# A hybrid decoder layer in fp32r on one core: the ConvFFN's gate and up products by one level of Strassen's scheme, the FFN in two passes through DRAM

## What is computed

```python
h = rmsnorm(x, norm_ffn_g)
gate, new_ffn = causal_dwconv(h @ w_gate, ffn_prev, conv_ffn_w, conv_ffn_b)
x = x + (jax.nn.silu(gate) * (h @ w_up)) @ w_down
```

## Time and profile before

| | us |
|---|---|
| median of 3 runs | 2509.6 (2509.47 to 2510.82) |
| span of the profiled execution | 2507.9 |
| PE busy (matmuls) | 2462.1, 98% |
| PE weight loads busy | 2452.1, 98% |
| DVE busy | 1206.8, 48% |
| ACT busy | 617.1, 25% |
| POOL busy | 160.2, 6% |
| mean granted clock of PE | 0.992 of full |
| DMA | 219.17 MB, mean 87 GB/s |

### The profile page before, as it was taken

How to read it: one execution, slowest core, us unless ns; L and a number is a source line. 1 busy time by engine, 2 the same in 40 slices (tenths; PEclk the granted TensorE clock), 3 DMA queues, 4 the chain that set the end, 5 groups by cost and what they waited for, 6 DMA issues and landing times.

```text
span 2507.9 us, 45612 instructions
## 1 busy us (share of the span) xinstructions
PE 2462.1 (98%) x18473; PEld 2452.1 (98%) x18473; DVE 1206.8 (48%) x1902; ACT 617.1 (25%) x738; POOL 160.2 (6%) x279
## 2 busy tenths in 40 slices
PE   6999999999999999999999999999999999999996
PEld 6999999999999999999999999999999999999996
DVE  6357644556224535455434444444544354454445
ACT  6224312113113322222212222122222211222224
POOL 3310000001221000000000000000000000000004
PEclk8999999999999999999999999999999999999998
DMA  5422222224222222223222222222232222222222
GB/s 153 159 84 71 69 85 85 83 85 151 83 79 73 84 80 81 84 84 92 75 84 84 84 84 81 80 80 82 78 97 78 76 84 84 84 84 84 84 85 84
DMA packets 326837, 219.17 MB, mean 87 GB/s; under 512 B 6804, under 2 KB 301839, under 8 KB 324992
## 3 DMA queue, kind: packets, MB, share of 16 engines
q1 hardware_dynamic: 324432, 203.98, 27.2%
q0 software_dynamic: 2352, 14.41, 1.6%
HBM read 208.19 MB, written 10.18 MB: 87 GB/s over the span
## 4 chain that ended last, share of the span: by engine, by line
PE 96%; ACT 1%; DVE 1%; POOL 0%; issue 0%; DMA 0%; POOLq 0%; SPq 0%; DVEq 0%; ACTq 0%
PE ps L1161 32%; PE ps L1163 31%; PE ps L1162 31%; DVE h_lo L797 0%; POOL acc L470 0%; ACT ps L540 0%; PE ps L1284 0%; ACT h_hi L512 0%; PE ps L1297 0%; DMA x_nat<-in_x_prompt_dram 0%; ACT X L520 0%; PE ps L1296 0%; ACT w_hi L491 0%; DVE rms L813 0%; PE ps L1276 0%
## 5 line engine op out<-in xcount | busy, mean ns | idle before, releaser
L1161 PE MATMUL ps<-h_hi,w_hi 128*128 128x288 f32 x4608 | 1362.2, 296 | 6.2 <-issue 4.9
L1163 PE MATMUL ps<-h_hi,w_lo 128*128 128x288 f32 x4608 | 1358.7, 295 | 0.0
L1162 PE MATMUL ps<-h_lo,w_hi 128*128 128x288 f32 x4608 | 1358.3, 295 | 0.0
L1161 PEld LDWEIGHTS ps<-h_hi,w_hi 128*128 128x128 f32 x4608 | 865.6, 188 | 8.4 <-issue 5.8
L1162 PEld LDWEIGHTS ps<-h_lo,w_hi 128*128 128x128 f32 x4608 | 865.7, 188 | 0.0
L1163 PEld LDWEIGHTS ps<-h_hi,w_lo 128*128 128x128 f32 x4608 | 865.7, 188 | 0.0
L771 DVE TENSOR_TENSOR w_lo<-raw,w_hi 128x1024 fp32r<-128x1024 f32 x376 | 460.5, 1248 | 305.7 <-ACT w_hi L491 305.6
L491 ACT ACTIVATE w_hi<-raw 128x1024 fp32r<-128x1024 f32 x376 | 384.2, 1050 | 489.9 <-PE ps L1163 474.5
L1161 PE MATMUL ps<-act_hi,w_hi 128*128 128x288 f32 x1408 | 418.4, 297 | 1.0 <-DVE scaled L781 1.0
L1163 PE MATMUL ps<-act_hi,w_lo 128*128 128x288 f32 x1408 | 415.0, 295 | 0.0
L1162 PE MATMUL ps<-act_lo,w_hi 128*128 128x288 f32 x1408 | 414.3, 294 | 0.0
(11 more groups left out here) (184 smaller groups left out, 921.6 us busy)
## 6 DMA issues: line engine op xcount, KB each, us to landing
raw<-in_w_gate_dram SPq DMA_DIRECT2D x88, 512.0 KB, 3.9
raw<-in_w_up_dram SPq DMA_DIRECT2D x88, 512.0 KB, 3.8
raw<-in_w_down_dram SPq DMA_DIRECT2D x88, 512.0 KB, 4.3
raw<-in_w_in_dram SPq DMA_DIRECT2D x80, 512.0 KB, 4.3
raw<-in_w_out_dram SPq DMA_DIRECT2D x32, 512.0 KB, 4.0
xT_scratch<-X POOLq DMA_DIRECT2D x1, 4608.0 KB, 18.5
X<-xT_scratch POOLq DMA_DIRECT2D x4, 1152.0 KB, 5.6
x_nat<-in_x_prompt_dram SPq DMA_DIRECT2D x4, 1024.0 KB, 8.6
```

Source lines behind the costliest of these rows:

```text
L1161: te.matmul(out, whi, xhi, start=start, stop=False)
L1162: te.matmul(out, whi, xlo, start=False, stop=False)
L1163: return te.matmul(out, wlo, xhi, start=False, stop=stop)
```

## The change

The FFN falls into two passes. Pass 1 computes gate and up of all 44 tiles and stores silu(gate)·up, split into hi and lo, in DRAM (`act_scratch`). Pass 2 reads that back in four chunks of 8, 12, 12 and 12 tiles and does the whole down projection: 24 groups of two output tiles, each over one chunk, and a last round over the fourth chunk that is interleaved with the final norm.

- **Tiles 0 to 3 of pass 1** are computed as before (`first_quad`, `std_quad`). h is now normalised fully before it is split: the sum of squares, the root, a reciprocal per half of the rows, then x·g·rb in place, the copy to hi and the subtraction. While these tiles run, DVE and ACT make the differences of row halves and contraction halves that the scheme needs, hi and lo, in `hq`, `tq` and in the place of X. X itself goes to DRAM first (`x2_scratch`, one DMA of POOL for each of its 16 rows) and comes back for the down projection.
- **Tiles 4 to 43** take one level of the Strassen-Winograd scheme over (gate, up) x (even, odd contraction tiles) x (row halves): 7 products of 8 steps and 3 matmuls, 168 matmuls of 128x288 for a gate and up tile, where it was 192 (`quad`, `product`). DVE adds four sums of weight pieces of 128x1024 (`sum1` to `sum4`), so that a tile has 7 pieces to split and 4 sums, from 4 loaded pieces. Intermediate sums of the outputs go through `snap` and `up_sum`.
- **The loads of a tile** are four of 512 KB: gate even and odd into `raw`, up even and odd into `raw_c` and `raw_d`. The two gate loads of the next tile wait until product 4 of this one has been split (both its buffers are in use up to there), the third until product 5, the fourth until product 6. In memory a piece now takes every second contraction tile (`wpart`), again in segments of 512 bytes.
- **POOL** stores each tile's activations (576 KB) with a DMA, in the same queue as its copies of convolution rows, and in pass 2 issues the loads of the chunks (2 tiles or 1152 KB each, the first two 4 tiles each).
- The pieces of w_down are now 512 contraction rows by 256 columns. The down projection has 4224 matmuls, before and after.
- The saved convolution rows are transposed in 9 matmuls instead of 20, and buffers have moved in SBUF.

```diff
-            with sp.Fori(1, NBLK) as b:
-                tile2(w_gate, b * 2, blk_q(b))
-                for d in range(4):
-                    load(blk_q(b) + 2 + d, d, down(b - 1, d))
-                tile2(w_up, b * 2, blk_q(b) + 6)
-                tile2(w_gate, b * 2 + 1, blk_q(b) + 8)
-                tile2(w_up, b * 2 + 1, blk_q(b) + 10)
...
+                if first:
+                    sp.wait_ge(lo_ready, n - 1)
+                else:
+                    sp.wait_ge(lo_ready, n - 2)
+                sp.dma_start(raw[:, 0], wpart(w_gate, f, 0)).then_inc(raw_landed[0], 16)
+                if first:
+                    sp.wait_ge(lo_ready, n)
+                sp.dma_start(raw[:, 1], wpart(w_gate, f, 1)).then_inc(raw_landed[1], 16)
...
+                    sp.wait_ge(lo_ready, n - 1)
+                sp.dma_start(raw_c[:, :, :], wpart(w_up, f, 0)).then_inc(c_landed, 16)
+                if not first:
+                    sp.wait_ge(lo_ready, n)
+                sp.dma_start(raw_d[:, :, :], wpart(w_up, f, 1)).then_inc(d_landed, 16)
...
+            q = D0
+            for f0, n in CHUNKS:
+                for g in range(KT // 2):
+                    for f in range(f0, f0 + n, 4):
+                        load(q, q % 2, down(f, g))
+                        q += 1
...
+            def spill(m, out):
+                g.dma_start(x2_scratch[:, ds(m * T, T)],
+                            X[:, ds(m, 1), :].rearrange("p a t -> p (a t)")).then_inc(out, 16)
...
+            def store_act(f):
+                pool.wait_ge(act_ready, f + 1)
+                g.dma_start(act_scratch[:, ds(f * (2 * T), 2 * T)],
+                            stage[:, :, :].bitcast(F32).rearrange("p s t -> p (s t)")).then_inc(act_stored, 16)
...
+            with pool.Fori(0, FT - 2) as f:
+                conv_pads(f + (HEADS + 1), ffn_state(f + 1))
+                store_act(f)
+                save_rows(f + (HEADS + 1), ffn_rows, f + 1)
...
+            for half in range(2):
+                for j in range(PJ):
+                    act.wait_ge(xn_ready, half * KT + 2 * j + 2)
+                    a.activation(hq[:, 2 * half:2 * half + 2, 0, j, :], X[:, 2 * j:2 * j + 2, half * HALF:(half + 1) * HALF],
+                                 ACT.Copy).then_inc(hqhi_ready, 1)
...
+                form_hi(i, u, 3)
+                if prev:
+                    silu(q - 1)
+                    s4(q - 1, n, 4 - b)
+                act.wait_ge(piece_done, n + 1)
+                act.wait_ge(z_ready, q + HEADS)
+                a.activation(snap[:, :], ps[:, b, 0:HALF], ACT.Copy).then_inc(s1_done, 1)
+                form_hi(i, u, 4)
+                form_hi(i, u, 5)
+                act.wait_ge(piece_done, n + 3)
+                act.wait_ge(act_prod, q)
+                a.activation(up_sum[:, HALF:T], ps[:, b + 1, 0:HALF], ACT.Copy).then_inc(s5_done, 1)
+                form_hi(i, u, 6)
+                if prev:
+                    act_hi_out(q - 1)
+                act.wait_ge(piece_done, n + 4)
+                act.wait_ge(c11_done, q - (STD - 1))
+                a.activation(snap[:, :], ps[:, b, 0:HALF], ACT.Copy).then_inc(s2_done, 1)
...
+                    for t in range(3):
+                        form_hi(*((i, u + 1) if u < 3 else (i + 1, 0)), t)
+                    tap2_ffn(q)
...
+            for half in range(2):
+                hs = slice(half * HALF, (half + 1) * HALF)
+                v.reciprocal(rb[:, hs], rms[:, hs]).then_inc(rrms_ready, 1)
+                dve.wait_ge(rrms_ready, 3 + KT + half)
...
+                    for k in (2 * j, 2 * j + 1):
+                        v.scalar_tensor_tensor(out=X[:, k, hs], in0=X[:, k, hs], scalar=vecs[:, G_FFN + k:G_FFN + k + 1],
+                                               in1=rb[:, hs], op0=ALU.mult, op1=ALU.mult).then_inc(xn_ready, 1)
+                    if j >= 1:
+                        pair_lo(j - 1)
...
-            with dve.Fori(1, NBLK) as b:
-                q, p, d = blk_q(b), blk_p(b), (b - 1) * 16
-                gate_in(b * 2, 0, p + 2)
...
-                for j in range(16):
-                    if j in (0, 2):
-                        split_lo(q + 4 + j // 2, j // 2)
-                    down_add(j, (j + 1) % 4, d + (j + 1))
...
+            def sum1(i, u):
+                dve.wait_ge(c_landed, cd_landed(i, u))
+                dve.wait_ge(d_landed, cd_landed(i, u))
+                v.tensor_tensor(raw_e[:, :, :], raw_c[:, :, :], raw_d[:, :, :], ALU.add).then_inc(sum_done, 1)
+            def sum3(i, u):
+                v.tensor_tensor(raw_c[:, :, :], raw[:, 0], raw_c[:, :, :], ALU.subtract).then_inc(sum_done, 1)
+            def sum2(i, u):
+                dve.wait_ge(sum_done, sums(i, u, 2))
+                v.tensor_tensor(raw[:, 0], raw_e[:, :, :], raw[:, 0], ALU.subtract).then_inc(sum_done, 1)
+            def sum4(i, u):
+                dve.wait_ge(sum_done, sums(i, u, 3))
+                v.tensor_tensor(raw[:, 1], raw[:, 1], raw[:, 0], ALU.subtract).then_inc(sum_done, 1)
...
+                form_lo(i, u, 3)
+                if prev:
+                    c21(q - 1, 4 - b)
+                    times_gate(q - 1)
+                form_lo(i, u, 4)
+                form_lo(i, u, 5)
+                dve.wait_ge(piece_done, n + 2)
+                dve.wait_ge(s1_done, q - (STD - 1))
+                v.tensor_tensor(zpad[:, 2:2 + HALF], ps[:, b + 2, 0:HALF], snap[:, :], ALU.add).then_inc(c11_done, 1)
...
+                form_lo(i, u, 6)
+                if not last:
+                    form_lo(*nxt, 0)
+                if prev:
+                    act_lo_out(q - 1)
+                if not last:
+                    form_lo(*nxt, 1)
+                    sum1(*nxt)
+                dve.wait_ge(piece_done, n + 5)
+                dve.wait_ge(s2_done, q - (STD - 1))
+                dve.wait_ge(rows_saved, q + HEADS)
+                m = SEQ - HALF
+                v.tensor_tensor(zpad[:, 2 + HALF:2 + SEQ], ps[:, b + 1, 0:m], snap[:, 0:m], ALU.add)
+                v.tensor_tensor(zs[:, :, 2:], samp8(ps[:, b + 1, m:HALF]), samp8(snap[:, m:HALF]),
+                                ALU.add).then_inc(z_ready, 1)
...
+                    sum3(*nxt)
+                    sum2(*nxt)
+                    form_lo(*nxt, 2)
...
+                dve.wait_ge(piece_done, n + 6)
+                dve.wait_ge(s5_done, q - (STD - 1))
+                v.tensor_tensor(up_sum[:, HALF:T], ps[:, b, 0:HALF], up_sum[:, HALF:T], ALU.add)
+                gate_conv(q)
+                if not last:
+                    sum4(*nxt)
...
-                pe.wait_ge(*((z_ready, HEADS + 1) if first else (down_added, d)))
-                gemm(q, 0, 0)
-                pe.wait_ge(act_ready, b * 2)
-                for j in range(16):
...
-                    down_tile((2 + j // 4) % 4, j % 4, (j + 1) % 4)
-                pe.wait_ge(down_added, d + 13)
-                gemm(q + 6, 2, 1)
...
+            def b_form(t, part, j):
+                if t < 2:
+                    return hq[:, t, part, j, :]
+                if t < 4:
+                    return tq[:, t - 2, part, j, :]
+                if t == 4:
+                    return hq[:, 3, part, j, :]
+                if t == 5:
+                    return Xr[:, 2 * j + part, part * HALF:(part + 1) * HALF]
+                return Xr[:, 2 * j + part, (1 - part) * HALF:(2 - part) * HALF]
...
+                for j in range(PJ):
+                    out = ps[:, bank, 0:HALF]
+                    te.matmul(out, w_hi[:, c, j, :], b_form(t, 0, j), start=start and j == 0, stop=False, skip_group_check=True)
+                    te.matmul(out, w_hi[:, c, j, :], b_form(t, 1, j), start=False, stop=False, skip_group_check=True)
+                    last = te.matmul(out, w_lo[:, c, j, :], b_form(t, 0, j), start=False, stop=stop and j == PJ - 1,
+                                     skip_group_check=True)
...
+                product(i, u, 0, b, True, False)
+                product(i, u, 1, b + 2, True, True)
+                if first and u == 0:
+                    pe.wait_ge(t_lo, 2)
+                product(i, u, 2, b + 1, True, False)
+                if first and u == 0:
+                    pe.wait_ge(t_lo, 4)
+                pe.wait_ge(s1_done, q - (STD - 1))
+                product(i, u, 3, b, False, False)
+                pe.wait_ge(s5_done, q - (STD - 1))
+                product(i, u, 4, b + 1, False, True)
+                if first and u == 0:
+                    pe.wait_ge(t_lo, 8)
+                pe.wait_ge(s2_done, q - (STD - 1))
+                product(i, u, 5, b, False, True)
+                product(i, u, 6, b + 3, True, True)
...
+            for gr in range(24):
+                ch, b = gr // 8, 4 * (gr % 2)
+                if gr >= 2:
+                    pe.wait_ge(down_added, gr - 1)
+                elif gr == 1:
+                    pe.wait_ge(rows_staged, 1)
+                first, last_m = group_piece(gr), group_piece(gr + 1) - 1
```

(12 more changed lines are left out.)

759 lines of the change are left out of this document (513 added, 246 removed).

## The result

The changed kernel takes **2394.45 us** (median of 4 runs, 2393.63 to 2397.22), the kernel before 2509.84 (2509.47 to 2510.82): a ratio of 0.9539 with a 95% interval of 0.9526 to 0.9552. That is 115 us less, where I forecast 52. It lies in my range, but it is rival A (2389, "the loads stay hidden"), not the forecast.

A forecast was written before the change was run, and what follows sets the result against it. PE, busy 98% of the span, was taken as the bound: 2507.9 - 127.3 + 7.7 + 0.9 - 2.1 = 2387.1 us, plus 68.4 for the load-DVE loop, 2455.5 of span, 2457 us as timed; range 2385 to 2495.

The forecast's parts named there:

- rival A: Strassen tiles: loads stay hidden if D is under 10.0 us, PE stays fed, 2389 us; chance 0.28.
- D: Strassen tiles: time from the split of product 4 to the fourth load's landing, taken as 11.8 us, between 8.8 and 12.8.
- Another load adds up to 2.6: Loads of a Strassen tile: one alone lands in 3.7 us, two in 6.3, so each further adds up to 2.6.
- The activation store falls into this stretch: Strassen tiles: POOL's store, issued about 7 us after the split of product 4, delays the loads by about 1.3 us.
- Some 1.2 and 2.8 us later: Strassen tiles: SP issues the up loads this long after the gate loads, following the splits of products 5 and 6.
- The loop: Strassen tiles: split of product 4, loads (D), then 12.3 us of DVE; tile 24.1 us, +68.4 us over 38 tiles.
- rival C: Strassen tiles: DVE's own work binds, sums taking 1.7 instead of 1.2 us each; 2465 us, chance 0.08.
- The worth of a matmul: Pass 1: each 128x288 matmul removed while PE stays fed saves 132.6 ns; 960 fewer give -127.3 us.
- the handover: Into the first Strassen tile: the sums wait for DVE's work on tile 3, +0.9 us.
- rival D: PE: the scheme saves no time because weight loads set the beat, so the 127.3 us would not come; no chance given.
- The way in: Start of the FFN: normalising ahead of the first product, with later start, hole and clock, costs +7.7 us together.
- the clock and the hole: Start of the FFN: +2.0 us for a lowered PE clock after idling, +2.1 us for PE's wait between row halves.

## Why the prediction was wrong

**The step that failed** is the price of D, "11.5 - 1.0 + 1.3 = 11.8". It measured 9.4. Two terms in it were too large by 1.3 us each, and both were needed for the error:

1. "Another load adds up to 2.6." Three of them less the 1.0 were 6.8 us; measured are 9.4 - 3.9 = 5.5, 1.8 for each. The 2.6 is 6.3 less 3.7, but the 3.7 is the time of another load, one alone. The pair's own first load took 4.8, so that by this row the second added 1.5. And the pair is not typical: of ten such pairs in the kernel before it has the deepest dip, 59 GB/s, and the slowest first load. I had written that "the dip stands in the row although the second load was already issued" and took it for a property of the queue. The wider spacing of its issues is a part of it: in the run with the gate loads apart D is 10.3.
2. "The activation store falls into this stretch": I had it 7 us after the split of product 4; it comes after 9, when the last load is all but landed. The 1.3 us were not there. As a price for a store that does fall among the loads they were fair: the run that put it there has 1.6.

The first load took 3.9 instead of 3.7, which gives 0.2 back: 11.8 - 1.3 - 1.3 + 0.2 = 9.4. "Some 1.2 and 2.8 us later" for the issue of the up loads was wrong too, without effect. The fourth was issued 4.5 us after the split of 4, since DVE waits 1.7 us for ACT ahead of the split of 6; but four loads issued within 2.3 us landed no earlier (9.3).

The loop was so near its threshold (22.27 - 12.3 = 10.0 in the forecast) that the 1.8 us of D beyond it were 68 us. Only one of the two terms put right would have left D at 10.5, and by the measured threshold of 22.39 - 12.2 = 10.2 a cost of some 11 us. The chance of 0.28 for rival A was about the share of my bounds, 8.8 to 12.8, that lay under 10.0; it was the bounds that were too high.

**What was right.** The loop itself: four runs that lengthen it are slower, tile by tile as D and DVE's work add up, and two that put the same work outside it or take work out of it are not. The 12.3 us of DVE in it (12.2). The price of a sum, taken from the split (1.21 to 1.23 us, four rows), so rival C fell: its 1.7 never appeared. The worth of a matmul, the handover, and the down pass without waits. To give rival D no chance was right too.

**The smaller terms.** The way in was 5.8 instead of 7.7 us: PE's start was 8.7 us after the last w_out matmul, within my 7 to 9, but I added the clock and the hole, and the run with the extra matmuls shows that one hides the other, because DVE paces the first tile. In the tail, PE's waits fell as expected, and 2.8 us came back behind the last transfer: its data end at 2387.0 and the program at 2392.2, before at 2505.5 and 2507.9. It is 5.2 to 5.4 us in the profiles of all edits to the changed kernel as well, so it belongs to the program and not to chance. What happens there no row shows.

**The rule of the Trainium skill** (DMA: Bandwidth & Descriptors, Anatomy of one DMA) gave four loads 6.8 us, by my estimate, and so a hidden loop. The page gives that fit for DMAs issued by GpSimd; these loads are issued by SP. The trace doesn't agree with the figure, 9.4 us measured. That the loop was hidden all the same is luck of that estimate: it had a margin of 3.2 us under the threshold, the measured loop has 0.8. The reason for which I set it aside, a row of 6.3 us for two loads, was read wrongly.

## What to carry to other kernels

A resource loop (buffer free, load, landing, work, buffer free) costs nothing up to its threshold and its full excess times the number of rounds beyond it: write down loop and beat side by side, and when they lie within a few per cent of each other, put the care into the bounds of the terms that decide between them. What a further transfer adds is the landing of the second less the landing of the first of the same pair, and a trace mostly has more than one such pair: look at all of them, and at those issued as the new code will issue them. When a loop is suspected, set the time of each round beside its variable part; here the single tiles of one trace say more than the averages of two. And before two small losses are added, ask whether the second is a wait for an engine that the first didn't slow down.

## What was not expected of the hardware

- Four loads of 512 KB in segments of 512 bytes in one queue, the first two issued 0.56 us apart, land 3.9, 5.8, 7.7 and 9.4 us after the first issue (medians of 37 tiles of the changed kernel): 1.8 us for each further one, whether the fourth is issued 2.3 or 4.3 us after the first. With the first two 1.1 us apart the last lands after 10.3 us. Single rounds take longer: up to 10.2 us in the changed kernel, up to 11.6 in the run with one extra instruction.
- A matmul of 128x288 of the same form takes 132.4 to 132.8 ns in most stretches and 133.25 in all seven products of the Strassen tiles, with PE always busy and at the full clock. It didn't change with 2.4 us more or 3.3 us less of DVE work per tile, and operands that both kinds of tile share are no faster in it. The last 42 w_out matmuls of the changed kernel also start 133.3 ns apart (783.64 to 789.24 us), so it is not a property of the Strassen tiles alone. It costs 4.4 us; its cause is open.
- In a stretch of 5.5 us in which PE was idle the granted clock fell: 0.61 in the mean of 794 to 796 us and 0.50 up to 800 us, so that 13 matmuls behind it ran at half speed. With most of that stretch filled by other matmuls the clock stayed at 1.00.
